# Partial sums of the spread modulation parts 16 to 23 on GpSimd instead of VectorE, with their folds two steps later

## The reference

```
sh1, sc1, g1, sh2, sc2, g2 = split(silu(c) @ w_ada + b_ada, 6)
h_l   = modulate(rms_norm(x, norm1_w), sh1, sc1)
mix_l = merge(h_l, gla_out(...), diff_out(...))      # w_gate, w_proj_gla, w_proj_diff, w_out
x_new = x + g1 * mix_l
h2_l  = modulate(rms_norm(x_new, norm2_w), sh2, sc2)
x_new = x_new + g2 * conv_ffn(h2_l, w_up, conv_w, conv_b, w_down)
# then the second layer (MLA, NSA and memory attention) and a final norm
```

## Time and profile before

| | us |
|---|---|
| runs | 2324.26, 2325.04, 2325.66, median 2325.04 |
| the profiled execution | 2324.98, its span 2323.2 |
| PE busy | 2240.4 (96%) |
| DVE busy | 1485.7 (64%) |
| ACT busy | 1038.5 (45%) |
| POOL busy | 47.3 (2%) |
| chain that ended last | PE 82%, DVE 7%, ACT 3%, DMA 3% |

### The profile page before, as it was taken

How to read it: one execution, slowest core, us unless ns; L and a number is a source line. 1 busy time by engine, 2 the same in 40 slices (tenths; PEclk the granted TensorE clock), 3 DMA queues, 4 the chain that set the end, 5 groups by cost and what they waited for, 6 DMA issues and landing times.

```text
span 2323.2 us, 37359 instructions
## 1 busy us (share of the span) xinstructions
PE 2240.4 (96%) x15465; PEld 2010.0 (87%) x15465; DVE 1485.7 (64%) x2116; ACT 1038.5 (45%) x1429; POOL 47.3 (2%) x61
## 2 busy tenths in 40 slices
PE   5899999999999999989999999999999999999997
PEld 2577777899888999779999988999978898999986
DVE  3346766387476478777888855566665644576664
ACT  3134343354555643344444433444454534454444
POOL 3000000021000000000000000000000000000000
PEclk9899999999999999999999999999999999999999
DMA  9956766454444578866778655555545566544454
GB/s 364 369 163 197 230 210 197 145 151 146 127 137 129 187 243 280 293 230 206 227 243 260 225 190 190 183 185 183 185 165 196 166 189 201 170 128 137 129 198 145
DMA packets 249738, 458.75 MB, mean 197 GB/s; under 512 B 18995, under 2 KB 43889, under 8 KB 248160
## 3 DMA queue, kind: packets, MB, share of 16 engines
q1 hardware_dynamic: 246496, 442.47, 58.7%
q0 software_dynamic: 2496, 9.69, 1.1%
q10 hardware_dynamic: 576, 4.19, 0.5%
HBM read 454.20 MB, written 2.10 MB: 196 GB/s over the span
## 4 chain that ended last, share of the span: by engine, by line
PE 82%; DVE 7%; ACT 3%; DMA 3%; DVEq 2%; issue 2%; SPq 1%; ACTq 0%
PE psum L648 73%; DVE fast L1921 2%; PE psum L625 2%; DVE sbuf L1973 2%; ACT fast L1324 1%; DMA sbuf<-in_w_ada 1%; PE psum L1157 1%; DVEq L1972 1%; PE psum L904 1%; PE psum L959 1%; PE psum L719 1%; DVE fast L1941 1%; DMA sbuf<-in_w_up 1%; PE psum L978 1%; PE psum L1187 1%
## 5 line engine op out<-in xcount | busy, mean ns | idle before, releaser
L648 PE MATMUL psum<-fast,fast 128*128 128x256 f32 (+1 forms) x13424 | 2034.2, 312 | 20.6 <-DVE fast L1921 14.4
L648 PEld LDWEIGHTS psum<-fast,fast 128*128 128x128 f32 x13424 | 1848.6, 191 | 195.4 <-issue 46.6
L1921 DVE TENSOR_TENSOR fast<-sbuf,fast 128x1024 fp32r<-128x1024 f32 (+5 forms) x685 | 784.0, 1152 | 678.5 <-ACT fast L1324 671.2
L1324 ACT ACTIVATE fast<-sbuf 128x1024 fp32r<-128x1024 f32 (+4 forms) x689 | 682.1, 998 | 1046.0 <-PE psum L648 911.5
L1973 DVE SCALAR_TENSOR_TENSOR sbuf<-sbuf,sbuf 128x512 f32<-128x512 f32 x210 | 157.8, 751 | 18.3 <-issue 0.5
L1324 ACT ACTIVATE sbuf<-psum 128x512 f32<-128x512 f32 (+4 forms) x193 | 85.6, 469 | 79.9 <-PE psum L648 33.3
L625 PE MATMUL psum<-sbuf,sbuf 128*128 128x128 f32 (+2 forms) x349 | 58.7, 284 | 22.3 <-DMA sbuf<-in_consts 10.5
L625 PEld LDWEIGHTS psum<-sbuf,sbuf 128*128 128x128 f32 (+2 forms) x349 | 42.7, 145 | 33.0 <-DMA sbuf<-in_consts 10.5
L1941 DVE TENSOR_TENSOR fast<-sbuf,fast 128x512 fp32r<-128x512 f32 (+1 forms) x61 | 53.4, 876 | 4.5
L1689 ACT ACTIVATE sbuf<-psum,sbuf 128x256 f32<-128x256 f32 x88 | 44.2, 552 | 0.0
L2352 DVE SCALAR_TENSOR_TENSOR sbuf<-psum,sbuf,sbuf 128x255 f32<-128x255 f32 x88 | 38.5, 478 | 3.6 <-issue 0.4
(11 more groups left out here) (263 smaller groups left out, 962.6 us busy)
## 6 DMA issues: line engine op xcount, KB each, us to landing
sbuf<-in_w_ada SPq DMA_DIRECT2D x192, 512.0 KB, 4.9
sbuf<-in_w_up SPq DMA_DIRECT2D x176, 512.0 KB, 4.4
sbuf<-in_w_in SPq DMA_DIRECT2D x154, 512.0 KB, 3.8
sbuf<-in_w_down SPq DMA_DIRECT2D x88, 512.0 KB, 4.3
sbuf<-in_w_gate SPq DMA_DIRECT2D x64, 512.0 KB, 3.6
sbuf<-in_w_out SPq DMA_DIRECT2D x64, 512.0 KB, 4.8
sbuf<-in_w_proj_gla SPq DMA_DIRECT2D x16, 512.0 KB, 4.7
sbuf<-in_w_proj_diff SPq DMA_DIRECT2D x16, 512.0 KB, 5.9
```

Of the source, the lines that this page charges most:

```text
L648: last = mm(out, lhsT, rhs, start=first and key not in opened, stop=end, skip_group_check=True)
L1324: return A(out, in_, ACT.Copy, scale=scale)
L1921: last = tt(lo, raw, hi.bitcast(F32), ALU.subtract)
```

## The change

On parts 16 to 23, VectorE no longer calls `sum_chunk`. GpSimd does the same sums with `tensor_tensor` alone: it multiplies the chunk in place by silu(c), laid out by a broadcast (128 x 1024), drains, and adds the two halves to the sums (two `tensor_tensor` of 128 x 512 with a drain between; one for the first chunk of a part), then gives `modulation_summed`. Parts 8 to 15 stay on VectorE. The calls stand between the waits and loads that GpSimd's queue has already: part 16 after the bias load, parts 17 and the first chunk of 18 after the loads of x, the rest of 18 and 19 after the loads of mem_2, parts 20 to 23 after the second bias load. The fold of these parts on TensorE is at s + 4 instead of s + 2, the keep on VectorE at s + 5 instead of s + 3.

```
--- before.py
+++ after.py
@@ -120,6 +120,7 @@
 
 IN2 = [("kc", 2880, 192), ("vc", 3072, 128), ("cq", 0, 512), ("ckv", 512, 512), ("krope", 1024, 64), ("qm", 4364, 512),
        ("qn0", 2112, 384), ("qn1", 2496, 384), ("ks", 3200, 192), ("kvw", 3392, 460)]
+SPREAD = 16
 O2_PAIRS = [6, 7, 4, 5, 0, 1, 2, 3]
 ZJOBS = [("z3", 4876, 512), ("z2", 3852, 512), ("z0", 1088, 512), ("z1", 1600, 512)]
 
@@ -263,7 +264,8 @@
                 self.sums_at.setdefault(s, []).append((a, i))
                 self.add(f"ada{a}", [ada[a][i]], 2)
                 if i == len(ada[a]) - 1:
-                    self.fold_at[s + 2] = self.keep_at[s + 3] = a
+                    f = s + (4 if a >= SPREAD else 2)
+                    self.fold_at[f] = self.keep_at[f + 1] = a
         assert not at
 
     def before(self, name):
@@ -574,17 +576,45 @@
                     pool.wait_ge(S("gla_scored"), 4 * 7)
                     nc.gpsimd.tensor_tensor(buf, gq, gq, ALU.add).then_inc(S("gla_queries"), 1)
 
+            def sum_chunks(a, first, final):
+
+                sums = rows[a % 2]
+                for i in range(first, final):
+                    g = st.job[f"ada{a}"][i]
+                    if i == 0:
+                        pool.wait_ge(S("ada_folded"), a - 1)
+                    if (a, i) == (SPREAD, 0):
+                        pool.wait_ge(S("modulation_summed"), st.nth[g])
+                    pool.wait_ge(S(st.landed(g)[0]), st.landed(g)[1])
+                    w = ring(g)
+                    nc.gpsimd.tensor_tensor(w, w, csil[:, 2 * i:2 * i + 2, 0:1].to_broadcast([P, 2, 512]), ALU.mult)
+                    pool.drain()
+                    if i == 0:
+                        last = nc.gpsimd.tensor_tensor(sums, w[:, 0, :], w[:, 1, :], ALU.add)
+                    else:
+                        nc.gpsimd.tensor_tensor(sums, sums, w[:, 0, :], ALU.add)
+                        pool.drain()
+                        last = nc.gpsimd.tensor_tensor(sums, sums, w[:, 1, :], ALU.add)
+                    last.then_inc(S("modulation_summed"), 1)
+
             pool.wait_ge(S("diff_pv_done"), 8)
             pool.dma_start(g1b, dram["b_ada"][0:1, 2 * D:3 * D].to_broadcast([P, D])).then_inc(S("spread_bias"), 16)
+            sum_chunks(16, 0, 8)
             pool.wait_ge(S("split_multiplied"), st.done("pg3")[1])
             pool.wait_ge(S("od_ready"), 2)
             for t in range(2):
                 pool.dma_start(x1[:, t, :], dram["x"][0, t * P:(t + 1) * P, :]).then_inc(S("x_back"), 16)
+            sum_chunks(17, 0, 8)
+            sum_chunks(18, 0, 1)
             pool.wait_ge(S("split_multiplied"), st.done("pd3")[1])
             for t in range(2):
                 pool.dma_start(memnat[t], dram["mem_2"][0, t * P:(t + 1) * P, :]).then_inc(S("mem_loaded"), 16)
+            sum_chunks(18, 1, 8)
+            sum_chunks(19, 0, 8)
             pool.wait_ge(S("x1_slices"), 8)
             pool.dma_start(g2b, dram["b_ada"][0:1, 5 * D:6 * D].to_broadcast([P, D])).then_inc(S("spread_bias"), 16)
+            for a in range(20, 24):
+                sum_chunks(a, 0, 8)
             pool.wait_ge(S("mem_ready"), 8)
             pool.dma_start(consts2, dram["consts"][:, NCONST1:NCONST]).then_inc(S("consts2_loaded"), 16)
             pool.wait_ge(S("g2_kept"), 4)
@@ -1975,7 +2005,8 @@
 
             def modulation(s):
                 for a, i in st.sums_at.get(s, ()):
-                    sum_chunk(a, i)
+                    if a < SPREAD:
+                        sum_chunk(a, i)
                 if 8 <= st.keep_at.get(s, 0) < 16:
                     columns_keep(st.keep_at[s])
                 if st.keep_at.get(s, 0) >= 16:
```

## The result

The changed kernel takes **2391.58 us** (median of 4 runs, 2381.02 to 2396.66) against 2325.35 before: ratio 1.0283, 95% interval 1.0265 to 1.0301. That is +66 us where +36 was forecast. The profiled execution has a span of 2391.9 us, 68.7 more than before.

The account below looks back on a forecast made before the run. The kernel was taken as a row of TensorE steps, where only what delays a step counts. +19 us for parts 16 to 19 and +17 for `w_up` gave +36 on 2324.98: 2361 us, range 2328 to 2435.

Parts of the forecast that it names:

- GpSimd's share of an op that runs beside VectorE: 1024-column multiply: of 2.41 us, some 0.58 of start passes beside VectorE and 1.83 of data excludes it.
- rival 1: GpSimd's whole op excludes VectorE, in the first stage (+54 us) and `w_up` (+56): 2435 us, chance 0.13.
- The chunk's pace: With a backlog on GpSimd, one chunk takes 6.6 us in pg and 6.7 in out.
- pd: VectorE is the bound in pd: 16.3 us per job of four steps, 7.6 us per chunk.
- The wait for pg3 ahead of the loads: GpSimd's queue, ahead of the loads of x: priced at nothing, up to 5.7 us if GpSimd is not behind.
- First stage: Parts 16 to 19 (pg, pd, out): out3's result read at 1043 instead of 1024.1, +19 us.
- `w_up`: Parts 20 to 23: +14 us from slots held longer and 3 for folds that wait, together +17.
- The four slots: `w_up` from uv1 on: chunks of sums hold slots 11.5 us, +2.4 us per 10 steps, +14 over 60 steps.
- Rate alone costs nothing here: `w_up`: a chunk takes 7.2 us of GpSimd where the steps give 7.2, so the pace itself loses nothing.
- Rival 2: The two engines' ops interleave without a gap lost, `w_up` stays even: +13 us, 2338 us, chance 0.16.
- Rival 3: Faster: collisions fall into VectorE's idle time and 8.2 us of stalls go, if chunks take under 6.2 us: 2317 us, chance 0.09.
- the signs in the profile: Expected afterwards: TensorE gaps of a fraction of a us to 2 us in most steps of pg to out3, among others.

Follow-up runs that it names:

- run 4: Changed kernel with GpSimd's multiply and adds replaced by memsets that read nothing and keep it busy about as long, sums left out: 2329.31 us, 1.0012.
- run 3: Changed kernel with GpSimd's drains between its own ops replaced by a semaphore that the op raises and the queue waits for: 2394.63 us, 1.0299.
- run 6: A fifth slot in the `w_up` stage, in the changed kernel: 2384.40 us, 1.0254; in the kernel before, as control: 2323.84 us, 0.9991.
- run 5: Changed kernel with the adds into the sums left out, GpSimd doing per chunk the 1024-column multiply and a small memset: 2332.90 us, 1.0036.

## Why the prediction was right or wrong

**Direction and mechanism: right.** It said that the reads of the two engines exclude each other, that sums of 1.6 us become a longer exclusive hold, and that TensorE stands behind VectorE's subtraction for it. Run 4 shows it by taking only the reads away. The size came out at 66 for 36 us, inside the stated range of 2328 to 2435, but with nearly twice the loss of its own 2361.

**GpSimd's share of an op that runs beside VectorE: wrong, and this is the term that was mis-sized.** The prediction took 0.58 us of start that passes beside VectorE and 1.83 us of data. It got the 0.58 by taking what was left of one op (L575, which adds a tensor to itself) from the mean of another (L572, 2.41, two different tensors). It also counted from the next op's start, 547.83; the subtraction ends at 547.90, which leaves 1.76. The changed kernel's multiply gives the same picture: issued just behind a subtraction's start it is recorded with 2.88 us and ends 1.76 after it, and undisturbed it takes 1.89. So the 1.76 is nearly all of an op, and rival 1's mechanism, that the whole op excludes, is what happens. (That L575 alone would also take 1.89 is argued: no trace has it undisturbed.) Rival 1's time wasn't reached: the multiply with the broadcast operand is 1.89 us instead of 2.41, and the add 1.27 instead of 1.50. The hold per chunk is 1.89 + 2 x 1.27 = 4.4 us, against 3.7 forecast and 5.4 in rival 1.

**The chunk's pace: right, by luck.** Forecast for out were 6.7 us from chunk to chunk with a backlog; 964.99 to 1004.17 is six chunks, 6.5 each. But 3.7 of hold was 0.7 too little, and the 1.125 x 0.68 = 0.8 added for gaps without a VectorE op made up for it (such a gap took 0.14); with the measured hold, 4.4 + 1.875 x 1.15 = 6.6 needs no such term. Alone a chunk would take 1.89 + 2 x 1.27 and two drains of 0.14, 4.7 us, less than the 5.35 that the steps allow and not more, as forecast: in these stages GpSimd is too slow only through VectorE.

**pd: the hold again.** It was put at 16.3 us per job of four steps, bound by VectorE; with the measured hold the same sum gives 9.8 + 2.13 x 4.4 - 1.4 = 17.8, and pd took 18.5 (877.64 to 951.69 for four). The section behind each job is eight short ops. Those that read PSUM keep their 0.68 us, as the -1.4 assumed. The others, the cast with its one input too, stand behind GpSimd's (0.69, 0.43 and 0.69 us before):

```profile
893.20 1.61 DVE L2317 TENSOR_TENSOR sbuf<-sbuf,sbuf 128x512 f32<-128x512 f32 x1
894.41 1.55 POOL L595 TENSOR_TENSOR sbuf<-sbuf,sbuf 128x512 f32<-128x512 f32 x1
894.89 1.35 DVE L1969 CAST fast<-sbuf 128x512 fp32r<-128x512 f32 x1
```

The wait for pg3 ahead of the loads was 0.8 us, as priced; the one for pd3 was 12.2, where 5.7 was the most. GpSimd was not four chunks behind: it had caught up with a pd that ran late.

**First stage: +37.4 for +19.** GpSimd keeps to the forecast up to the end of pg. It begins the last 15 chunks at 952.8 instead of 940.5, since pd is 9 us too long and GpSimd waits for it; they take 102.3 us instead of 99, with a drain of 7.4 among them that was not foreseen; and from its last sum (1055.08) to VectorE's reading of out3 (1061.47) it is 6.4 us instead of 3.7. These are the 18 us. They are not to be had from GpSimd's side, though: run 3 took 9 of them out of its row and won nothing. The forecast also had no term for the clock. TensorE was busy 9.5 us longer in this stage and 9.9 in `w_up`, over a quarter of the loss, and the clock was lower in and behind the long gaps. In run 4, where the gaps in the first stage are 2.6 us at most, the matmuls are busy 2034.6 us, as before.

**`w_up`: +30.2 for +17, and the reason given was a quarter of it.** The four slots were to cost 14; by run 6 they cost 7 or 8. "Rate alone costs nothing here" rested on the 3.7 us of hold: 3.7 + 3 x 1.15 = 7.2 in 7.2 us of steps. With 4.4 it is 7.9. All of it goes away with the reads (run 4: 725.6 us from the second norm to the constants' load, 726.0 in the kernel before), so it is exclusion, but the 23 us or so beside the slots have no single place: TensorE's gaps of 1 to 4 us lie behind subtractions that stood behind GpSimd's ops in VectorE's own order. That this is where they arise is argued from the trace; no run takes VectorE's other ops out of the order, and none gives a sixth slot.

**The rivals.** Rival 2 (no gap lost) had about the right pace too, 198 us for 30 chunks, 6.6 each. It fell with what it made of it: +13 where the first stage alone lost 37, and `w_up` was not even. Rival 3 (faster) fell with the pace: its point of decision was 6.2 us. In runs 4 and 5 the chunk is shorter than that, and even there 4 and 8 us are lost, not won. Of the signs in the profile, TensorE's gaps were to be up to 2 us in most steps; they were fewer and longer, 56.5 us in 20 waits of up to 10.5.

## What to carry to other kernels

Before an op with SBUF inputs goes to GpSimd, add up how long its reading ops and VectorE's ops with two SBUF inputs take in the stage, whole ops on both sides, and compare the sum with the length of the stage (here 6.7 us in 5.35 lost much, 4.2 in 5.35 little): a busy share of 2% on GpSimd is not free capacity while VectorE does two-input work. Take the length of an op from rows of that very op, not from a difference between two. An engine that is overloaded in one short stage is relieved more cheaply by moving the work in time (here 5.6 us faster) than to the engine whose reads exclude its own (66 us slower). And a hole in an engine's row, however long, is worth only what the next engine waits for it.

## What the runs showed of the hardware that was not expected

- GpSimd's `tensor_tensor` of 128 x 1024 took 1.89 us with one operand broadcast along the row (the changed kernel, L590) and 2.41 with both full (the kernel before, L572); 128 x 512 with both full took 1.27 (L597).
- A drain on GpSimd behind two of its own loads of 1 MB each took 9.45 and 7.37 us, with a compute op between load and drain (8.50 in run 4, behind a memset); a wait for that op's own semaphore took under 0.1 (run 3).
- GpSimd's memsets leave VectorE's subtractions at 1.23 us (run 4). The Trainium skill's page SBUF — State Buffer, section Who interferes with whom, has this as a rule (two SBUF inputs contend with a GpSimd op that reads SBUF, not with one that only writes). This run agrees; and its "fully blocks", which the prediction had weighed down by the earlier trace rows, is what both directions show: 1.08 of 1.23 us and 1.76 of 1.89 us were left after the other's end.
- VectorE's cast within SBUF, with one input, stood behind GpSimd's ops as well: 0.43 us before, a median of 1.35 in pd of the changed kernel. Its ops with one input in PSUM kept their 0.68.
- TensorE's granted clock was 1.00 up to a gap of 10.5 us, fell to 0.50 inside it, was still 0.50 in the first 2 us of matmuls behind it and 1.00 some 6 us after they began. Behind the gaps of 6.9 and 3.8 us it was 0.50 and 0.57 in the first 3 to 4 us.
